# Delta-rule inverse: four projection heads and the query-key product placed between the widths of the inverse

## What is computed

```python
kk = jnp.einsum('nbhik,nbhjk->nbhij', k_beta, kc) * seg
a_mat = jnp.eye(L) + jnp.where(strict, kk, 0.0)
sol = lax.linalg.triangular_solve(a_mat, rhs, left_side=True, lower=True)
u, w = sol[..., :V], sol[..., V:]
attn = jnp.einsum('nbhik,nbhjk->nbhij', qc, kc) * seg      # query-key product, masked and decayed
def step(S, xs):                                           # chunk after chunk
    v_new = u_c - w_c @ S
    o = q_d @ S + a_c @ v_new
    S = S * exp(bl) + k_o^T @ v_new
y = (rms_norm(o) * silu(z)) @ w_out                        # output projection
x = x + gate * rms_norm(y)
```

## Time and profile before

| | |
|---|---|
| Median of three runs | 2462.7 us (2458.26 to 2464.17) |
| Profiled execution, its own time | 2462.23 us |
| its span, first to last instruction | 2460.5 us |
| TensorE busy in the span | 95% |
| VectorE, ScalarE, GpSimd busy | 59%, 39%, 35% |
| mean granted clock of TensorE | 0.973 of 2.4 GHz |
| last stage (`phase_mix_c`) | from about 1653 us to the end |
| a tile of it, from tile 2 on | 43.6 us |

### The profile page before, as it was taken

How to read it: one execution, slowest core, us unless ns; L and a number is a source line. 1 busy time by engine, 2 the same in 40 slices (tenths; PEclk the granted TensorE clock), 3 DMA queues, 4 the chain that set the end, 5 groups by cost and what they waited for, 6 DMA issues and landing times. The chain is left out here.

```text
span 2460.5 us, 56669 instructions
## 1 busy us (share of the span) xinstructions
PE 2328.8 (95%) x22052; PEld 1662.4 (68%) x22052; DVE 1459.9 (59%) x3102; ACT 951.9 (39%) x2661; POOL 871.0 (35%) x1090
## 2 busy tenths in 40 slices
PE   6999999998899998899999999987999999999997
PEld 2444444444556643688888887876888878888785
DVE  3343647460677865677685775565565665656655
ACT  3544454434111113344443434334444544445431
POOL 1552323223111110123131221017566565665652
PEclk8999999999899998899999999998999999999997
DMA  9453675855554445886776666646332232322213
GB/s 308 136 177 113 214 207 180 238 161 163 177 209 153 153 130 189 291 278 201 220 233 192 200 199 209 182 121 195 87 112 70 87 96 71 113 62 88 79 40 90
DMA packets 372159, 395.13 MB, mean 161 GB/s; under 512 B 39600, under 2 KB 263024, under 8 KB 371939
## 3 DMA queue, kind: packets, MB, share of 16 engines
q1 hardware_dynamic: 337826, 360.28, 46.7%
q10 hardware_dynamic: 34112, 31.71, 4.2%
HBM read 275.19 MB, written 116.72 MB: 159 GB/s over the span
## 5 line engine op out<-in xcount | busy, mean ns | idle before, releaser
L2792 DVE SCALAR_TENSOR_TENSOR inc_acc<-inc_ub,inc_taps,inc_acc 128x512 f32<-128x512 f32 x288 | 245.4, 852 | 10.7 <-ACT inc_acc L2632 3.8
L758 PE MATMUL inab_b<-inab_wt,keep 128*128 128x512 f16 x768 | 166.7, 379 | 1.7 <-POOL inab_wt L575 1.7
L758 PE MATMUL inab_b<-inab_wt,raw_next 128*128 128x512 f16 x768 | 166.4, 379 | 0.0
L2569 POOL COPY inc_halo<-inc_ub 128x3 f32<-128x3 f32 x96 | 48.9, 510 | 317.2 <-DVE inc_ub L2780 180.7
L1390 PE MATMUL mixab_y<-keep,mixab_oT_hi 128*128 128x512 f16 x512 | 153.6, 382 | 7.0 <-DVE mixab_f_y L1470 5.3
L739 POOL TENSOR_TENSOR inab_a_out<-inab_stage,inab_a_out 128x384 f16<-128x384 f32 x64 | 67.6, 1056 | 209.7 <-ACT inab_a_out L730 209.7
L758 PEld LDWEIGHTS inab_b<-inab_wt,keep 128*128 128x128 bf16 (+1 forms) x768 | 75.1, 98 | 91.1 <-issue 1.9
L758 PEld LDWEIGHTS inab_b<-inab_wt,raw_next 128*128 128x128 bf16 (+1 forms) x768 | 75.1, 98 | 90.0
L2636 ACT ACTIVATE inc_acc<-inc_acc 128x512 f32<-128x512 f32 x96 | 60.5, 630 | 141.1 <-DVE inc_acc L2792 140.7
L2908 PE MATMUL inc_b<-inc_room,keep 128*128 128x256 bf16 (+3 forms) x864 | 110.1, 281 | 2.7 <-DVE stage_next L2762 2.7
L3285 POOL TENSOR_TENSOR mixc_levels<-mixc_BT,raw_next 128x512 f32<-128x512 f32 (+1 forms) x82 | 110.2, 1375 | 1.5 <-DVE mixc_BT L3571 1.5
(11 more groups left out here) (621 smaller groups left out, 6191.7 us busy)
## 6 DMA issues: line engine op xcount, KB each, us to landing
keep<-tmp_w SPq DMA_DIRECT2D x336, 256.0 KB, 3.4
tmp_qkv<-inc_acc SPq DMA_DIRECT2D x96, 256.0 KB, 3.0
inab_stage<-in_w_in_c SPq DMA_DIRECT2D x128, 128.0 KB, 2.6
tmp_w<-inab_stage SPq DMA_DIRECT2D x64, 256.0 KB, 3.2
inab_stage<-in_w_in_ab ACTq DMA_DIRECT2D x24, 512.0 KB, 4.0
tmp_w<-inab_a_out SPq DMA_DIRECT2D x64, 192.0 KB, 2.6
stage_next<-in_w_ada ACTq DMA_DIRECT2D x6, 2048.0 KB, 14.7
raw_next<-tmp_qkv SPq DMA_DIRECT2D x8, 1536.0 KB, 6.8
```

The costliest lines, as they stand in the source:

```text
L758: last = nc.tensor.matmul(dst, lhs(a, k), rhs(b, k), start=(k == 0 and i == 0), stop=(k == KT - 1 and i == len(PASSES) - 1))
L2569: pool.tensor_copy(halo[:, g, :], ub[w % 2][side][:, BLK:]).then_inc(halo_saved[side], 1)
L2792: ins = dve.scalar_tensor_tensor(a_v, u_[:, i:i + BLK], taps[:, g, i:i + 1], a_v, ALU.mult, ALU.add)
```

## The change

Four things move, all in the last stage.

- The query-key product of a tile leaves the end of the tile before (and the prologue) and is cut into four parts of two heads. Group 0 goes into bank `B[1]` in width 2, group 1 into `A[1]` in width 3; one part stands in front of the group-0 products, the other behind the second y group.
- Heads 4 and 5 of the projection's second half leave the tile's end. The four heads 4 to 7 now stand at the four corresponding places of widths 0 and 1.
- VectorE's `attention` goes into widths 3 and 4, where `gated` stood; `gated` goes behind the second sum of the same width.
- ScalarE's square of the projection goes from width 0 to width 1, since the projection ends later.

The waits follow: the first products of a tile wait for the query squares that read `B[0]`, and `turn_k` of group 1 for the first attention alone. The end of the last tile, which prepares the sample tokens, stays as it was. Group 0 keeps both of its products.

```diff
+    QK = (B[1], A[1])
@@ ScalarE, body
-                if k == 0 and early >= 2:
+                if k == 1 and early >= 2:
                     fin.square(act, t - 2, P, 1)
@@ VectorE, levels
             for k in range(1, len(widths)):
                 y_part(t, k, 0, halves, widths)
                 n_part(t, k - 1, 1, halves, widths)
-                beside(k)
+                between(k)
                 n_part(t, k, 0, halves, widths)
                 y_part(t, k, 1, halves, widths)
+                after(k)
@@ VectorE, body
+            def between(k):
+                if k >= 3:
+                    attention(t, par, P, k - 3, QK[k - 3])
+
+            def after(k):
+                if k >= 3 and early >= 2:
+                    gated(t - 2, P, k - 3)
@@ TensorE, query_keys
+        def query_keys(t, par, n, g, bank, part=(0, 1)):
+
+            if 0 in part:
+                pe.wait_ge(q_sq, nth(t, 1))
+            for i, h in heads(g):
+                if i // 2 in part:
+                    last = mm(bank[0:n, i, 0:n], qkv[par][:, 8 + h, 0:n], qkv[par][:, h, 0:n], start=True, stop=True)
+            if 1 in part:
                 last.then_inc(qk_done, 1)
@@ TensorE, levels
             y_product(t, 0, 1, halves, widths)
-            beside(0)
-            pe.wait_ge(attn_ready, nth(t, 1))
+            beside(0, 0)
+            pe.wait_ge(q_sq, nth(t, 0))
             tn_products(t, 0, 0, halves, widths)
-            beside(1)
+            beside(0, 1)
             for k in range(1, len(widths)):
                 y_product(t, k, 0, halves, widths)
                 tn_products(t, k - 1, 1, halves, widths)
+                beside(k, 0)
                 tn_products(t, k, 0, halves, widths)
                 y_product(t, k, 1, halves, widths)
-            beside(2)
+                beside(k, 1)
@@ TensorE, body
-            def beside(k):
+            def beside(k, part):
                 if k < 2 and t >= 2:
-                    fin.project(pe, t - 2, P, 1, [6 + k])
-                if k == 2:
+                    fin.project(pe, t - 2, P, 1, [4 + 2 * k + part])
+                if k in (2, 3):
+                    query_keys(t, par, P, k - 2, QK[k - 2], (part,))
+                if k == 4 and part == 1:
                     turn_k(t + 1, nxt, half, n2, 1)
...
                 fin.project(pe, t - 1, P, 1, range(0, 4))
-            query_keys(t + 1, nxt, n2)
-            if t >= 1:
+            if t == nt - 1:
+                for g in GRP:
+                    query_keys(t + 1, nxt, n2, g, B[g])
                 fin.project(pe, t - 1, P, 1, range(4, 6))
```

More of the change, by code:

```diff
@@ L3585, in key_products, with attention @@
                               ).then_inc(t0_ready, 1)
[L3587 to L3590, removed]
+        def attention(t, par, n, g, bank):
+            dve.wait_ge(qk_done, nth(t, g))
+            dve.tensor_tensor(attn[0:n, gs(g), 0:n], bank[0:n, :, 0:n], seg[par][0:n, gs(g), 0:n], ALU.mult).then_inc(attn_ready, 1)
         def y_part(t, k, g, halves, widths):
@@ L3610, in n_part, with levels @@
                 dve.tensor_copy(N[HALF[1], gs(g), HALF[1]], LN[g][HALF[1]]).then_inc(n_high, 1)
-        def levels(t, halves, widths, beside=lambda k: None):
+        def levels(t, halves, widths, between, after):
             y_part(t, 0, 0, halves, widths)
@@ L3684, in body @@
             nxt = 1 - par
-            levels(t, BOTH, LEVELS, (lambda k: gated(t - 2, P, k - 3) if k in (3, 4) else None) if early >= 2 else (lambda k: None))
+            def between(k):
[4 more added lines that the diff above has]
+                    gated(t - 2, P, k - 3)
+            levels(t, BOTH, LEVELS, between, after)
             if early >= 1:
@@ L3700, in body @@
                 dve.tensor_copy(attn[HALF[1], :, 0:NS], bc(tv["eye_h"][HALF[1]].unsqueeze(1), [HB, H, NS]))
-            attention(t + 1, nxt, n2)
+                for g in GRP:
+                    attention(t + 1, nxt, n2, g, B[g])
         key_products(0, 0, P, BOTH)
         scaled_values(0, P)
-        attention(0, 0, P)
         body(0, 0, 0)
@@ L3798, in turn_k @@
             if t and g == 1:
-                pe.wait_ge(attn_ready, nth(t - 1, 1))
+                pe.wait_ge(attn_ready, nth(t - 1, 0))
             elif t:
@@ L3996, in _ @@
         turn_q(0, 0, P)
-        query_keys(0, 0, P)
         pe.wait_ge(init, 1)
```

## The result

The changed kernel takes 2472.79 us (median of 17 runs, 2466.39 to 2480.69), the kernel before 2459.96 (17 runs, 2456.11 to 2466.91). The ratio is 1.005, with a 95% interval of 1.004 to 1.006: 12.8 us slower. The profiled execution took 2472.22 us with a span of 2470.5, 10.0 more than the span of before.

A forecast was written before the change was run, and what follows sets the result against it. TensorE was taken to bound the last stage; per tile 1.49 + 2.58 - 3.09 = +0.98 us, in sum 15.5 us on 2462.23, giving 2477.7 us. The range was 2468 to 2486, the forecast's own 2473 to 2482 at 0.69.

The forecast's parts named there:

- The fill's price: Widths, TensorE: going from 64x64 blocks to a full 128x128 matmul and back costs 0.225 us a fill, read from width 0.
- The extra 0.10 of a query-key fill: Widths 2 and 3: each query-key fill costs another 0.10 us for entry, taken from the sample part.
- The second rival: Query-key fills in widths 2 and 3: the extra 0.10 us is not paid, 6.4 us less, 2471 us; chance 0.13.
- The pair: Two query-key fills in one width, 2 or 3, cost TensorE 1.29 us; two such pairs in a tile cost 2.58.
- the first rival: Fills in widths 1 to 3: entry and exit are free, hidden in the 0.13 us waits; 2451 us, chance 0.07.
- The estimate from that page's drain: Fills on TensorE: about 128 cycles a drain, 0.11 us a pair of mode changes, +0.27 a tile, some 2467 us.
- What leaves the end: Tile's end, TensorE: without the query-key product and two projection heads the next first width starts 3.09 us earlier.
- VectorE in width 4: Width 4's first sum, now behind a gated product, still ends 0.26 us before TensorE delivers, at no cost.
- The third rival: Width 4: VectorE's chain becomes the bound, its excess over 0.26 us paid in every tile; 2485 us and up, chance 0.11.
- The whole: Entire kernel: 13.7 us for tiles 2 to 15, +2.6 for tile 0, -0.8 for tile 1, so 15.5 us slower.

The follow-up runs named there:

- the run with two fills: Changed kernel with each query-key pair in one fill instead of two, so two fills fewer in a tile: 2468.07 us, ratio 1.0029 against the kernel before.
- the split of the N products: Kernel before with group 0's N products moved behind the second y group in widths 1 to 3, into free bank B[1]: 2456.58 us, ratio 0.9987.
- the fastest kernels: Kernel before with group 0's N products behind the second y group, plus both gated products late (2454.24 us) or only the second (2454.56 us).
- the first three experiments: Projection heads alone moved in the kernel before, 1.0011; changed kernel with projection put back, 1.0039; changed kernel with one fill per query-key pair, 1.0029.

## Why the prediction was right, and where it was not

**The fill's price** (0.225, from width 0) was right: width 1 lasts 4.18 where 2.69 + 1.49 was said. **The extra 0.10 of a query-key fill** was paid: in the records of each such fill the first takes 0.213 us until the next, the others 0.112. The second rival falls. The pair cost 1.25 to 1.26 where 1.29 was said. That entry and exit cost more than the wait they replace, the run with two fills shows; the first rival falls. The Trainium skill, "TensorE: Matmul & The Clock Gate", section "The mechanism", would have a weight load pulled ahead of running matmuls where their row groups do not conflict, or where it goes into the background buffer; across the change of tiling mode this trace doesn't show it (0.213 against 0.112). The estimate from that page's drain would have given +0.27 a tile; it was +0.96.

**What leaves the end** was right: from the first y group of width 4 to the next tile, 31.82 became 28.74 to 28.82, 3.04 less on average for 3.09 said. Tile 1 starts 0.22 us behind VectorE's state update (1714.10 + 1.12 = 1715.22; the earlier trace rows have 3.48): 3.26 sooner for 3.4 said. The tile came out at +0.96 for +0.98, and tile 15 at +4.0 (1.49 + 2.58 for its own fills; my sum counted tile by tile, with the end of the tile before it, which comes to the same total).

**VectorE in width 4** held as said: 0.26 us to spare in the sum, 0.31 in the trace. The third rival didn't happen, but its mechanism is real: with the cover gone (one fill in place of two, or the gated products late with no fill at all) it costs what the gap shows, 0.23 us. One thing I had not seen: moving the second gated product was a gain. It gave 0.08 us here (the gap ahead of the last products fell from 0.47 to 0.39), since attention took the place, and 0.27 where nothing did.

**The whole** is where a step failed: 12.8 us measured, 15.5 summed. The forecast of 2477.7 was 4.9 too high. 2.3 of that is the point from which it was counted: the profiled execution's 2462.23 against a median of 2459.96 over 17 runs. The other 2.7 points to a term that I left out, the stalls. I read the earlier trace rows as one gap of 0.2 us in each tile "of which a single one is 3.6" and put no price on either; in truth two of the sixteen are stalls. I took tile 0's 46 us for the clock. TensorE in before, tile 0, products of width 2, and below it the changed kernel at the same place:

```profile
1684.73 0.41 PE L3876 MATMUL mixc_C<-mixc_levels,mixc_N 64*64 64x64 f32 x6
1688.77 0.79 PE L3876 MATMUL mixc_C<-mixc_levels,mixc_N 64*64 64x64 f32 x9 [3.63 <-issue]
```

```profile
1685.94 0.63 PE L3890 MATMUL mixc_C<-mixc_levels,mixc_N 64*64 64x64 f32 x14
1688.49 0.33 PE L3890 MATMUL mixc_C<-mixc_levels,mixc_N 64*64 64x64 f32 x2 [1.92 <-issue]
```

A stall in the midst of sixteen equal records, 3.85 us from start to start before and 2.14 after. In the two traces tile 0 holds 5.6 us of them before and 2.6 after, tiles 2 to 14 lose 2.3 before and nothing after. The profile's balance of 10.0 us is: start of tile 0 +1.1, tile 0 -4.8, tile 1 -0.3, tiles 2 to 14 +10.1, tile 15 +4.0, sample part -0.1. My sum, cut in the same way, is 0, -0.8 (2.58 - 3.4), -0.5 (2.58 - 3.09), +12.7 (13 x 0.98), +4.1 and 0. The start is inherited from the stages ahead (1670.8 to 1676.8 in the traces of this study). The rest of the gap, 4.0 in tile 0 and 2.6 in tiles 2 to 14, stands beside 3.0 and 2.3 us of stalls that went. The granted clock in tile 0 rose too, from 0.88 to 0.92. It differs most behind the stall, 0.76 against 1.00, the upper of the two levels (columns as in the earlier trace rows; before, and below it the changed kernel):

```profile
1689.00:1700.00 11.00, 11.00 (x190) 10.46 (x189) 5.04 (x9) 7.23 (x23) 4.25 (x2) 0.76 0.01 4
```

```profile
1689.00:1700.00 11.00, 10.89 (x197) 9.79 (x197) 6.93 (x11) 8.00 (x31) 4.25 (x2) 1.00 0.01 4
```

As an estimate from the means of the tile the clock is worth some 2.2 us (46.0 x 0.12 - 41.2 x 0.08), if TensorE lost by it all along. No run took stalls and clock apart, and the balance is one trace of each kernel; the second trace of before loses 0.8 in tiles 2 to 14, not 2.3. So that the stalls are the missing 2.7 fits, but is not shown.

## What to carry to other kernels

A fill between small matmuls has a price for entry and exit that does not depend on its length (0.225 us here, 0.10 more for f32 blocks of 128; one fill of eight records in place of two of four saved one entry and exit): it pays where the wait is longer than that (0.35 and 0.64 in width 0), not where it is 0.165. Fill few places with much, and look first for a reordering that takes the wait away, as the split of the N products did. And an "issue" wait in the profile is worth a look before it is left out of a sum: here it hid a wait for VectorE in each tile from tile 2 on, and stalls that no record of another engine explains.

## What the runs showed of the hardware

TensorE's stalls look like waits for its own instructions. In all thirteen traces, every stall of over 0.4 us inside a group of equal records in tiles 0 to 15 ends 1.2 to 1.6 us after a packet of 16,384 bytes has landed on the DMA queue for instructions. Five packets come in a tile, 3.5 to 22 us apart, so that by chance about one stall in twenty would end in such a stretch of 0.4 us. (The sample part of three traces has one gap of 0.66 us without such a packet.) In before's tile 0 the packet started at 1686.30 and took 1.09, so it landed at 1687.39; TensorE went on at 1688.77, 1.38 later. In the changed kernel it started at 1686.13 and took 1.04; TensorE went on at 1688.49, 1.32 later. The page's part 3 has the queue (packets, MB, share), and the DMA view of tile 6 alone in the changed kernel below it:

```profile
q8 instruction: 163, 2.67, 0.4%
```

```profile
q8 instruction: 5, 0.08, 0.8%
```

Five packets in a tile of 625 matmuls and 624 weight loads: 250 instructions a packet, without the waits. The Trainium skill, "Advanced Engine Details and Errata", section "ISA Cache", has lines of 16 KB that hold 256 instructions; this trace's packets agree with it.

So a stretch of small matmuls uses up a packet faster than the tile's mean of 8.9 us: a width of 2.51 us in the split kernels holds 80 matmul records and as many weight loads, so 250 of them in 3.9 us (an estimate from these counts). Widths 1 to 4 of the fastest kernels are such a stretch, and there the stalls are: 9 of 13 steady tiles have one of over 0.4 us in the run with the split and the second product late, 4 with two more fills in width 1, 5 in the run without fills in width 0, at most 2 in the two traces of before, none in the changed kernel and in the first three experiments, which have more fills than before. That the density is the cause fits all of these, though no run changed the instructions alone, so neither that nor the wait for instructions is shown by itself. It limits what a tighter order can still give: the split and the late products take 0.78 us off a clean tile, 10 us in 13 tiles, and the kernel gains 6.3.
